# A new order of history copies, token sums, weight parts and snapshots around a blocked FFN-up product

## The chip, the cores and the metric

The kernel runs on one core of a Trainium2 chip. The metric is the device time of one execution in microseconds (us), given as the median of several runs. PE is the matmul engine (TensorE), DVE is VectorE, ACT is ScalarE, POOL is GpSimd, SP issues the weight DMAs.

## What is computed

Two layers of a streaming encoder over 512 prompt frames and 32 sample frames, handled together as 544 columns. Each layer has three gated branches (convolution, spatial gating, stick-breaking attention), an output projection with a layer norm, and then this channel mixer, in which the whole change lies:

```python
f_gate, f_val = jnp.split(x @ w_up, 2, axis=-1)          # 1024 -> 2 * 2816
ffn_ext = jnp.concatenate([ffn_hist, f_gate], axis=1)    # two frames of history
f = gelu(causal_dwconv(ffn_ext, ffn_conv_w, ffn_conv_b)) * f_val   # 3 taps
x = layer_norm(DN_ALPHA * x + f @ w_down, ln2_g, ln2_b)
```

## The kernel before

**Number format.** Every large product is made of three matmuls: an operand is split into a high part (ACT copies it to fp32r: `wh`, `xh`, `th`, `shi`, `fhh`) and a low part (DVE subtracts the high part from the raw value: `wl`, `xl`, `tl`, `slo`, `fll`). PE multiplies high by high, low by high and high by low. A weight chunk comes by DMA into one of three ring slots `raw`; `hi()` and `lo()` make its two parts (the low part takes the place of the raw values), and PE frees the slot when its last unit is read. The 544 columns are two halves of 272.

**The FFN-up product.** 22 gate tiles and 22 value tiles of 128 channels are made in pairs. The first two pairs of each are plain chunks: s0 (gate 0), s1 (value 0), s2 (gate 1), and one last plain chunk, value 1, which is the `chunk()` ahead of the blocked part. The other 18 weight chunks are 18 blocks q (`QUADS`), a gate chunk and a value chunk in turn, so that two blocks make one pair of tiles. A block is a 2 x 2 block product done with seven products (q,1) to (q,7) of 12 matmuls each instead of eight, in the Strassen-Winograd manner. Their order on PE is written out in `ORDER`: (q,3), (q,4), (q,5), (q+1,1), (q,6), (q+1,2), (q,7). For this

- POOL makes four sums of the activations once a layer (`traw` T1, T3, T2, T4N), and four sums of the weights for each block (`sums`, L558: s1, a21 in place, s2, s4);
- ACT makes their high parts (`turned_x_hi`, L979; `first_blocks`, `two_sums`, `last_sum`, L1007), and snapshots of PSUM banks between products (`snapshot`, L1012: m1, u1, u3), which PE must not overwrite before;
- DVE makes the low parts (`turned_x_lo`, L1791; `first_low`, L1798; `other_lows`, L1809: the second half of the weights, then `slo` in two pieces) and combines banks and snapshots (`bottom_right` c22, `left` c11 and c21, L1831). (q,7) waits for c22 of its block.

**Convolution of the gate.** `history` (DVE, L1764) puts two history columns into `gex`; `first_tap`, or `conv_open` (L967) for the plain pairs, applies the first tap on ACT; `conv_close` (DVE, L1746) the other two, with two small copies; ACT applies gelu; DVE multiplies with the values (`f_products`, `gated_values`). `gate_rows` (ACT, L962) copies plain gate rows from PSUM to `gex` and frees the bank.

**Down projection.** f is split by `f_his` (ACT, L1041) and `f_lows` (DVE, L1785) in six groups of tiles for each half of the columns. `down(h)` runs over six weight chunks, twice for each half; chunk j waits for its low part and for the f groups that it covers.

**What sets the order.** There is no planner: each engine has its own instruction list, written out in the code, and runs it strictly in that order; semaphores tie the lists together. An instruction that waits holds up all behind it on its engine.

## Time and profile before

| | us |
|---|---|
| median of three runs | 1814.01 (1813.14 to 1819.28) |
| the profiled execution, whole | 1812.31 |
| its span, first to last instruction | 1810.6 |
| PE busy | 1754.7 (97%) |
| DVE busy | 1348.9 (75%) |
| ACT busy | 850.5 (47%) |
| POOL busy | 345.0 (19%) |
| mean granted clock of PE | 0.991 |

The profile is of one execution. A row of the timeline gives start, length, engine, line, instruction, output and inputs, and in brackets how long the engine had been idle and what released it. The ends of matmuls are modelled and overlap, so the starts are the better guide: at full clock they are some 0.125 us apart. The granted clock is given as a share of 2.4 GHz; its other level is 1.2 GHz.

### The profile page before, as it was taken

To read this page: it belongs to the slowest core of one execution; us is meant where nothing else is said; L and a number is where in the kernel's file an instruction comes from. 1 tells how busy PE (TensorE), PEld (TensorE's weight loads), DVE (VectorE), ACT (ScalarE), POOL (GpSimd) and SP (SyncE) were. 2 spreads that over 40 slices of the span, in tenths; PEclk is the share of its full clock that TensorE was granted. 3 is DMA by queue.
4 is the path that set the end of the run, shared out by engine and by line. 5 is a ranking of instruction groups with operands and counts; after the bars stand their busy time and mean duration, and the time that the engine had idled before them with its cause. 6 is when DMAs were issued, how large, how long until landed. Compare 5 with 4: busy or idle time off the path is not lost.

```text
span 1810.6 us, 32645 instructions
## 1 busy us (share of the span) xinstructions
PE 1754.7 (97%) x13802; PEld 1709.7 (94%) x13802; DVE 1348.9 (75%) x1869; ACT 850.5 (47%) x1366; POOL 345.0 (19%) x311
## 2 busy tenths in 40 slices
PE   9999999999999999999999999999999999998997
PEld 9998999999999999999999989999999989998997
DVE  5798777755778888866668886786558778887665
ACT  4256523353455555544552564324535555555443
POOL 0034000000144455200000350000001545551000
PEclk9999999999999999999999999999999999999999
DMA  4522122223222222245525221222232222222544
GB/s 170 168 95 71 59 72 82 94 82 128 71 71 70 94 93 85 92 154 180 170 96 168 75 92 40 80 94 82 94 105 70 76 88 94 94 81 97 177 167 137
DMA packets 36514, 186.00 MB, mean 103 GB/s; under 512 B 7376, under 2 KB 11728, under 8 KB 18192
## 3 DMA queue, kind: packets, MB, share of 16 engines
q1 hardware_dynamic: 34672, 176.28, 29.0%
q10 hardware_dynamic: 1696, 7.64, 1.2%
q8 instruction: 109, 1.79, 0.4%
q14 instruction: 37, 0.30, 0.1%
HBM read 176.75 MB, written 7.15 MB: 102 GB/s over the span
## 4 chain that ended last, share of the span: by engine, by line
PE 74%; DVE 12%; issue 4%; DMA 4%; ACT 3%; POOL 3%; ACTq 0%; DVEq 0%; POOLq 0%
PE acc L1978 21%; PE acc L1984 20%; PE acc L1983 20%; DMA raw<-wup 3%; PE score L1978 2%; DVE slo L1818 2%; PE score L1984 2%; PE score L1983 2%; POOL sraw L569 1%; PE score L2054 1%; DVE wl L1199 1%; PE small L2105 1%; PE turned L2085 1%; DVE wl L1813 1%; DVE cbuf L1753 1%
## 5 line engine op out<-in xcount | busy, mean ns | idle before, releaser
L1978 PE MATMUL acc<-xh,wh 128*128 128x272 f32 x1936 | 570.6, 295 | 14.0 <-ACT gex L962 6.4
L1984 PE MATMUL acc<-xh,wl 128*128 128x272 f32 x1936 | 560.9, 290 | 0.0
L1983 PE MATMUL acc<-xl,wh 128*128 128x272 f32 x1936 | 559.9, 289 | 0.0
L1978 PEld LDWEIGHTS acc<-xh,wh 128*128 128x128 f32 x1936 | 367.5, 190 | 22.4 <-issue 18.3
L1199 DVE TENSOR_TENSOR wl<-raw,wh 128x2048 fp32r<-128x2048 f32 (+2 forms) x118 | 236.0, 2000 | 179.4 <-ACT wh L601 178.8
L1983 PEld LDWEIGHTS acc<-xl,wh 128*128 128x128 f32 x1936 | 367.7, 190 | 0.1
L1984 PEld LDWEIGHTS acc<-xh,wl 128*128 128x128 f32 x1936 | 366.7, 189 | 0.0
L601 ACT ACTIVATE wh<-raw 128x2048 fp32r<-128x2048 f32 (+2 forms) x138 | 236.4, 1713 | 169.1 <-DMA raw<-wdn 122.4
L1978 PE MATMUL acc<-fhh,wh 128*128 128x272 f32 x704 | 205.5, 292 | 6.2 <-DVE wl L1199 6.2
L1983 PE MATMUL acc<-fll,wh 128*128 128x272 f32 x704 | 203.5, 289 | 0.0
L1984 PE MATMUL acc<-fhh,wl 128*128 128x272 f32 x704 | 202.8, 288 | 0.0
L1403 DVE SCALAR_TENSOR_TENSOR acc<-glu,par,acc 128x574 f32<-128x574 f32 x240 | 181.0, 811 | 0.1
L1978 PEld LDWEIGHTS acc<-fhh,wh 128*128 128x128 f32 x704 | 133.2, 189 | 7.7 <-DVE wl L1199 7.3
L879 ACT ACTIVATE tmp<-acc,par 128x272 f32<-128x272 f32 x96 | 46.6, 488 | 195.5 <-PE acc L1984 195.2
L1984 PEld LDWEIGHTS acc<-fhh,wl 128*128 128x128 f32 x704 | 133.3, 189 | 0.0
L1983 PEld LDWEIGHTS acc<-fll,wh 128*128 128x128 f32 x704 | 133.0, 189 | 0.2
L546 POOL TENSOR_TENSOR wl<-raw,wh 128x512 fp32r<-128x512 f32 x8 | 11.3, 1440 | 593.2 <-ACT wh L601 593.2
L569 POOL TENSOR_TENSOR sraw<-raw 128x512 f32<-128x512 f32 x36 | 60.6, 1685 | 204.3 <-DMA raw<-wup 158.1
L1978 PE MATMUL score<-th,shi 128*128 128x272 f32 x288 | 85.4, 297 | 2.2 <-ACT u L1016 2.2
L1984 PE MATMUL score<-th,slo 128*128 128x272 f32 x288 | 83.5, 290 | 0.0
L1983 PE MATMUL score<-tl,shi 128*128 128x272 f32 x288 | 83.0, 288 | 0.0
L1818 DVE TENSOR_TENSOR slo<-sraw,shi 128x1024 fp32r<-128x1024 f32 x72 | 78.6, 1132 | 1.1 <-ACT shi L1005 1.1
(322 smaller groups left out, 4178.0 us busy)
## 6 DMA issues: line engine op xcount, KB each, us to landing
raw<-win SPq DMA_DIRECT2D x50, 1024.0 KB, 5.0
raw<-wup SPq DMA_DIRECT2D x44, 1024.0 KB, 4.9
raw<-wdn SPq DMA_DIRECT2D x32, 1024.0 KB, 4.9
raw<-wbr SPq DMA_DIRECT2D x24, 512.0 KB, 3.6
raw<-wdn SPq DMA_DIRECT2D x16, 768.0 KB, 4.2
raw<-wout SPq DMA_DIRECT2D x8, 1024.0 KB, 4.9
v_out<-vfm ACTq DMA_DIRECT2D x2, 1088.0 KB, 9.2
k_out<-k ACTq DMA_DIRECT2D x2, 1088.0 KB, 4.9
```

Source lines behind the costliest of these rows:

```text
L569: g.tensor_tensor(s1, a21, a22, ALU.add).then_inc(s_made, 1)
L601: A(wh[s][:, 0:n], raw[s][:, 0:n], ACT.Copy).then_inc(hi_full[s], c.up(hi_full[s]))
L879: A(tmp[:, b, :], ps[b][:, 0:HALF], ACT.Sigmoid, bias=col(par, PAR["b_gate"] + 8 * BRANCHES[n] + 2 * i + b % 2)).then_inc(acc_free[b], c.u ...
L1199: v.tensor_tensor(wl[s][:, 0:n], raw[s][:, 0:n], wh[s][:, 0:n].bitcast(F32), ALU.subtract).then_inc(lo_full[s], c.up(lo_full[s]))
L1403: v.scalar_tensor_tensor(out=acc[:, m, :], in0=glu_at(m, j), scalar=w, in1=acc[:, m, :], op0=ALU.mult, op1=ALU.add).then_inc(vec, c.up(vec))
L1753: v.scalar_tensor_tensor(out=cbuf[:, m, :], in0=gex[:, m, 1:GEX - 1], scalar=col(par, PAR["fw"] + FT + t), in1=cbuf[:, m, :], op0=ALU.mult ...
L1813: v.tensor_tensor(wl[s][:, n:], raw[s][:, n:], wh[s][:, n:].bitcast(F32), ALU.subtract).then_inc(lo_full[s], c.up(lo_full[s]))
L1818: v.tensor_tensor(slo[i][:, part, :], sraw[i][:, part, :], shi[i][:, part, :].bitcast(F32), ALU.subtract).then_inc(s_ready, 1)
L1978: first = mm(out, a, xs[0], start=start, stop=False, skip_group_check=onto)
L1983: mm(out, a, xs[1], start=False, stop=False, skip_group_check=onto)
L1984: return mm(out, b, xs[0], start=False, stop=stop, skip_group_check=onto)
L2054: last = mm(bs[b][:, 0:w], yc[x][rows, ht, i * P:w], ks[y][rows, ht, 0:w], start=x + y == 0, stop=y == 1)
```

## The change

It alters the written-out orders of ACT and DVE around the blocked part, one bank, and the waits of PE that go with it.

- Entry, ACT: the second pair's gate rows come ahead of the activation sums' high parts, which are made two (T2, T3) and later two (T1, T4N); the first taps of pair 1 (`conv_taps`) come ahead of block 0's weight parts, and the gelus of pair 1 behind block 0's sums.
- Entry, DVE: `history(1)` ahead of the last plain low part; two activation low parts; both tap groups of pair 1; then block 0's low parts, then the two other activation low parts. PE waits for each activation sum alone, where it is first used.
- Product (0,2) goes to the bank `bt` (`bank_of`), so it does not wait for the value products of pair 1; (1,2) and (2,2) do, and (1,4) waits for c11 of block 0.
- Loop, DVE: the history copy of the next pair comes right behind c11 of the even block instead of behind `other_lows` of the odd one; it also waits on `conv3_full`, which DVE's own taps raise.
- Loop, ACT: `last_sum(q + 1)` comes behind the snapshot u1 and, in odd q, behind the first taps.
- Exit: the first high and low parts of f move into the last turn of the loop, the down projection's second weight chunk is split ahead of the last gated values (DVE) and of f's third group; in the second half, each weight part comes ahead of the f part that it was behind.

```diff
--- before.py
+++ after.py
@@ -204,6 +204,7 @@
         TB = 4 * HALF * 4
         T2, T3, T1, T4N = range(4)
+        T_PLACE = {T2: 1, T3: 2, T1: 3, T4N: 4}
         th = [sb(f"th{j}", [P, 4, HALF], F32R, at=F + 2 * FB + 2 * j * TB) for j in range(4)]
         tl = [sb(f"tl{j}", [P, 4, HALF], F32R, at=F + 2 * FB + (2 * j + 1) * TB) for j in range(4)]
         traw = [sb(f"traw{j}", [P, 4, HALF], at=F + 2 * FB + (2 * j + 1) * TB) for j in range(4)]
@@ -371,6 +372,11 @@
         cbank = (bo, bt)
         PA, PB, PC = (ps[0], ps[1]), (bs[0], bs[1]), (bo, bt)
+        def bank_of(q, p):
+            if p == 2:
+                return PA[q % 2] if q else PC[1]
+            return (PC if p in (4, 7) else PB)[q % 2]
+
         def full_at(l, q, p):
             return l * len(ORDER) + PLACE[q, p]
@@ -964,21 +970,17 @@
                         A(gex[:, m, 2 + HALF:2 + SEQ], bank[:, 0:BP], ACT.Copy)
                         A(gex[:, m, 4 + SEQ:GEX], bank[:, BP:HALF], ACT.Copy).then_inc(acc_free[b], c.up(acc_free[b]))
-                def conv_open(i, later=0):
-
-                    act.wait_ge(acc_free[3], c.seen(acc_free[3], 1 if later else 0))
+                def conv_taps(i):
+                    act.wait_ge(acc_free[3], c.seen(acc_free[3]))
                     act.wait_ge(gex_full, c.take(gex_full, 2))
                     for m in range(2):
                         t = 2 * i + m
                         A(cbuf[:, m, :], gex[:, m, 0:GEX - 2], ACT.Identity, scale=col(par, PAR["fw"] + t),
                                    bias=col(par, PAR["fb"] + t)).then_inc(tap0_full, c.up(tap0_full))
-                    for m in range(2):
-                        act.wait_ge(conv3_full, c.take(conv3_full))
-                        A(cbuf[:, m, :], cbuf[:, m, :], ACT.Gelu).then_inc(fgelu_full, c.up(fgelu_full))
-
-                def turned_x_hi():
-                    for n, j in enumerate((T1, T3, T2, T4N)):
-                        act.wait_ge(t_made, 4 * l + n + 1)
+
+                def turned_x_hi(*js):
+                    for j in js:
+                        act.wait_ge(t_made, 4 * (l + 1))
                         A(th[j][:, :, :], traw[j][:, :, :], ACT.Copy).then_inc(t_hi, 1)
                 def chunk_of(q):
@@ -1053,22 +1055,29 @@
                 norm_out(1, "ln1_g", "ln1_b")
                 gate_rows(2, bs[0])
                 gate_rows(3, bs[1])
-                conv_open(0)
+                conv_taps(0)
+                conv_gelu(0)
+                conv_gelu(1)
                 hi()
                 for b in range(4):
                     c.skip(acc_full[b])
                     c.skip(acc_free[b])
-                turned_x_hi()
-                second_blocks(0)
-                for b in range(4):
+                for b in range(2):
                     gate_rows(b, SECOND_GATE[b])
+                turned_x_hi(T2, T3)
+                for b in range(2, 4):
+                    gate_rows(b, SECOND_GATE[b])
+                conv_taps(1)
                 for b in range(4):
                     c.skip(acc_full[b])
                     c.skip(acc_free[b])
+                second_blocks(0)
                 first_blocks(0)
-                conv_open(1, 1)
                 two_sums(0)
                 last_sum(0)
+                turned_x_hi(T1, T4N)
+                conv_gelu(0)
+                conv_gelu(1)
                 for q in range(QUADS + 1):
                     if q:
                         snapshot("u3", q - 1, 5, "c22")
@@ -1076,24 +1085,25 @@
                     if q < QUADS:
                         snapshot("m1", q, 1, "c11")
                     else:
-                        f_his(0, 1)
+                        f_his(0, 0)
                     if q and q % 2 == 0:
                         conv_gelu(0)
                     if q:
                         top_right(q - 1)
+                    if q == QUADS:
+                        f_his(0, 1)
                     first_blocks(q + 1)
                     if q and q % 2 == 0:
                         conv_gelu(1)
                     two_sums(q + 1)
-                    last_sum(q + 1)
                     if q == QUADS - 1:
                         hi()
                     if q < QUADS:
                         snapshot("u1", q, 3, "c21")
                     if q % 2:
                         first_tap(q - 1)
-                    if q == QUADS - 1:
-                        f_his(0, 0)
+                    last_sum(q + 1)
+                hi()
                 f_his(0, 2)
                 hi()
                 for g_ in range(3, 6):
@@ -1105,7 +1115,7 @@
                         hi()
                 final = l == DEPTH - 1
-                his(2)
+                his(1)
                 f_his(1, 0)
                 his(1)
                 f_his(1, 1)
@@ -1114,8 +1124,8 @@
                 his(1)
                 skip(range(4))
                 for g_ in range(3, 6):
+                    his(1)
                     f_his(1, g_)
-                    his(1)
                 his(1)
                 square_first(0)
                 his(2)
@@ -1763,6 +1773,8 @@
                 def history(i):
+                    if c.seen(conv3_full):
+                        dve.wait_ge(conv3_full, c.seen(conv3_full))
                     for m in range(2):
                         ins = v.tensor_copy(gex[:, m, 2 + SEQ:4 + SEQ], row(fhist, 2 * i + m, 0, 2))
                         ins.then_inc(gex_full, c.up(gex_full))
@@ -1788,10 +1800,10 @@
                     v.tensor_tensor(fll[h][:, a:b, :], f32[h][:, a:b, :], fhh[h][:, a:b, :].bitcast(F32),
                                     ALU.subtract).then_inc(f_ready, c.up(f_ready))
-                def turned_x_lo():
+                def turned_x_lo(*js):
                     dve.wait_ge(t_made, 4 * (l + 1))
-                    for n, j in enumerate((T1, T3, T2, T4N)):
-                        dve.wait_ge(t_hi, 4 * l + n + 1)
+                    for j in js:
+                        dve.wait_ge(t_hi, 4 * l + T_PLACE[j])
                         v.tensor_tensor(tl[j][:, :, :], traw[j][:, :, :], th[j][:, :, :].bitcast(F32),
                                         ALU.subtract).then_inc(t_ready, 1)
@@ -1830,7 +1842,7 @@
                 def left(q, m):
                     i = 2 + q // 2
-                    bank, add = (PA[q % 2], snap[q % 2]["m1"]) if m == 0 else (PC[q % 2], snap[q % 2]["u1"])
+                    bank, add = (bank_of(q, 2), snap[q % 2]["m1"]) if m == 0 else (PC[q % 2], snap[q % 2]["u1"])
                     dve.wait_ge(prod_full, full_at(l, q, 7 if m else 2))
                     dve.wait_ge(snapped, act_at(l, "u1" if m else "m1", q))
                     out = gex[:, m, 2:2 + HALF] if q % 2 == 0 else f32[0][:, 2 * i + m, :]
@@ -1850,36 +1862,41 @@
                 history(0)
                 conv_close(0)
                 f_products(0, FIRST_VALUE)
+                history(1)
                 lo()
-                turned_x_lo()
-                history(1)
-                first_low(0)
+                turned_x_lo(T2, T3)
                 skip(range(4))
                 conv_close(1, range(2), False)
+                first_low(0)
                 other_lows(0)
+                turned_x_lo(T1, T4N)
                 f_products(1)
+                history(2)
                 for q in range(QUADS + 1):
                     if q:
                         bottom_right(q - 1)
+                    if q == QUADS:
+                        f_lows(0, 0)
                     if q and q % 2 == 0:
                         conv_close(1 + q // 2, (1,), False)
                     if q < QUADS:
                         left(q, 0)
+                        if q and q % 2 == 0:
+                            history(2 + q // 2)
                     first_low(q + 1)
                     if q:
                         left(q - 1, 1)
+                    if q == QUADS:
+                        f_lows(0, 1)
+                        lo()
                     if q and q % 2 == 0:
                         gated_values(q - 1)
                     if q == QUADS - 1:
                         lo()
                     other_lows(q + 1)
                     if q % 2:
-                        history(2 + q // 2)
                         conv_close(2 + q // 2, (0,), False)
-                    if q == QUADS - 1:
-                        f_lows(0, 0)
-                for g_ in range(1, 3):
-                    f_lows(0, g_)
+                f_lows(0, 2)
                 lo()
                 for g_ in range(3, 6):
                     f_lows(0, g_)
@@ -1889,7 +1906,7 @@
                         lo()
                 final = l == DEPTH - 1
-                los(2)
+                los(1)
                 f_lows(1, 0)
                 los(1)
                 f_lows(1, 1)
@@ -1900,8 +1917,8 @@
                     residual(b, b, 0)
                 shift_sum(0)
                 for g_ in range(3, 6):
+                    los(1)
                     f_lows(1, g_)
-                    los(1)
                 centre(0)
                 lo()
                 squares_open()
@@ -2335,7 +2352,7 @@
                 def products(n):
                     q, p = ORDER[n]
-                    bank = {1: PB, 6: PB, 7: PC, 2: PA, 3: PB, 4: PC, 5: PB}[p][q % 2]
+                    bank = bank_of(q, p)
                     sums = 2 * (r * QUADS + q)
                     if p == 1:
                         blocks[q] = arrived()
@@ -2345,13 +2362,15 @@
                         pe.wait_ge(lo_full[blocks[q]], c.take(lo_full[blocks[q]]))
                         if q > 1:
                             pe.wait_ge(combined, dve_at(r, "c11", q - 2))
-                        else:
-                            pe.wait_ge(acc_free[q], c.seen(acc_free[q]))
+                        if q in (1, 2):
+                            pe.wait_ge(acc_free[q % 2], c.seen(acc_free[q % 2]))
                     if p == 3:
                         pe.wait_ge(snapped, act_at(r, "m1", q))
                         pe.wait_ge(s_ready, sums + 1)
-                        if q == 0:
-                            pe.wait_ge(t_ready, 4 * (r + 1))
+                    if p in (3, 4, 5, 7) and q == 0:
+                        pe.wait_ge(t_ready, 4 * r + T_PLACE[{3: T2, 4: T3, 5: T1, 7: T4N}[p]])
+                    if p == 4 and q == 1:
+                        pe.wait_ge(combined, dve_at(r, "c11", 0))
                     if p == 4 and q > 1:
                         pe.wait_ge(combined, dve_at(r, "c21", q - 2))
                     if p == 5:
```

## Rows read from the trace of the kernel before

**Rows 1.** The page: busy time, share of the span and instructions of each engine.

```profile
PE 1754.7 (97%) x13802; PEld 1709.7 (94%) x13802; DVE 1348.9 (75%) x1869; ACT 850.5 (47%) x1366; POOL 345.0 (19%) x311
```

**Rows 2.** The waits of PE: who for, us in total, times, longest.

```profile
PE score L1978 <- ACT u L1016: 21.4, 18, 2.5
PE acc L1978 <- ACT gex L962: 6.4, 2, 3.2
...
```

**Rows 3.** Timeline of PE: start, us, instruction, in brackets idle time before and releaser.

```profile
536.87 0.57 PE L1978 MATMUL acc<-xh,wh 128*128 128x272 f32 x1 [3.21 <-ACT gex L962]
...
555.82 0.36 PE L1978 MATMUL acc<-xh,wh 128*128 128x272 f32 x1 [2.51 <-DVE f L1777]
...
646.59 0.40 PE L1978 MATMUL score<-xh,shi 128*128 128x272 f32 x1 [1.14 <-ACT u L1016]
...
770.69 0.39 PE L1978 MATMUL acc<-fhh,wh 128*128 128x272 f32 x1 [2.12 <-DVE wl L1199]
...
806.28 0.39 PE L1978 MATMUL acc<-fhh,wh 128*128 128x272 f32 x1 [0.75 <-DVE wl L1199]
```

**Rows 4.** Stretches: length, PE, PEld, DVE, ACT, POOL busy (x), PEclk, DMA, GB/s.

```profile
521.47:533.49 12.02, 12.02 (x98) 11.96 (x96) 9.45 (x15) 8.45 (x11) 5.68 (x3) 1.00 0.51 174
536.87:551.64 14.77, 14.77 (x97) 14.77 (x97) 14.70 (x14) 4.02 (x9) 11.78 (x7) 0.80 0.21 72
646.59:669.79 23.20, 21.97 (x168) 21.31 (x168) 20.46 (x29) 12.86 (x22) 12.25 (x9) 1.00 0.26 93
770.69:780.00 9.31, 9.31 (x62) 9.31 (x63) 6.85 (x5) 3.42 (x3) 0.00 (x0) 0.82 0.39 124
```

**Rows 5.** Timeline of ACT at the entry.

```profile
531.40 4.09 ACT L982 ACTIVATE th<-traw 128x1088 fp32r<-128x1088 f32 x4
```

**Rows 6.** Timeline of DVE at the entry.

```profile
533.74 9.21 DVE L1795 TENSOR_TENSOR tl<-traw,th 128x1088 fp32r<-128x1088 f32 x4
...
544.11 1.21 DVE L1806 TENSOR_TENSOR wl<-raw,wh 128x1024 fp32r<-128x1024 f32 x1
```

**Rows 7.** Timeline of POOL at the entry.

```profile
542.48 1.62 POOL L569 TENSOR_TENSOR sraw<-raw 128x512 f32<-128x512 f32 x1 [0.68 <-DMA raw<-wup]
```

**Rows 8.** Timeline of ACT in a pair of blocks.

```profile
644.68 1.58 ACT L1034 ACTIVATE cbuf<-gex,par 128x546 f32<-128x546 f32 x2 [3.33 <-DVE gex L1767]
646.17 0.37 ACT L1016 ACTIVATE u<-score 128x272 f32<-128x272 f32 x1
```

**Rows 9.** Timeline of PE, first matmuls of (7,7) and (8,7).

```profile
649.98 0.39 PE L1978 MATMUL turned<-th,wh 128*128 128x272 f32 x1
...
660.93 0.29 PE L1978 MATMUL small<-th,wh 128*128 128x272 f32 x1
```

**Rows 10.** Timeline of DVE in the same pair.

```profile
644.34 0.23 DVE L1767 COPY gex<-fhist 128x2 f32<-128x2 f32 x2
...
647.87 1.71 DVE L1759 SCALAR_TENSOR_TENSOR cbuf<-gex,par,cbuf 128x546 f32<-128x546 f32 x1
...
649.50 0.43 DVE L1829 TENSOR_TENSOR f<-turned,u 128x272 f32<-128x272 f32 x1
...
651.49 0.79 DVE L1759 SCALAR_TENSOR_TENSOR cbuf<-gex,par,cbuf 128x546 f32<-128x546 f32 x1
...
656.63 2.92 DVE L1818 TENSOR_TENSOR slo<-sraw,shi 128x1024 fp32r<-128x1024 f32 x2
...
659.48 0.40 DVE L1826 TENSOR_TENSOR gex<-small,u 128x240 f32<-128x240 f32 x1
```

**Rows 11.** Timeline of POOL in the same pair.

```profile
644.72 1.28 POOL L569 TENSOR_TENSOR sraw<-raw 128x512 f32<-128x512 f32 x1 [4.62 <-DMA raw<-wup]
...
657.02 1.98 POOL L569 TENSOR_TENSOR sraw<-raw 128x512 f32<-128x512 f32 x1 [6.30 <-DMA raw<-wup]
```

**Rows 12.** Timeline of DVE at the end of the blocked part.

```profile
765.94 2.48 DVE L1788 TENSOR_TENSOR fll<-f,fhh 128x1088 fp32r<-128x1088 f32 x2
...
768.35 2.28 DVE L1199 TENSOR_TENSOR wl<-raw,wh 128x2048 fp32r<-128x2048 f32 x1
```

## The prediction

> **What bounds the kernel now.** I read the page's busy line first, then who PE waits for, then PE's instructions that follow an idle stretch, then the stretches around them. PE is busy for 1754.7 us, 97% of the span [rows 1], so an edit of order can only win idle PE time and the time in which PE runs below its full clock. The list of waits puts nearly all of the idle time in the blocked FFN-up part and its two ends [rows 2]: 21.4 us on ACT's snapshots in 18 waits and 6.4 us on ACT's gate rows in 2. In a layer these are: 3.21 us before the last plain value chunk, 2.51 us before product (0,2), 1.14 us before the sixth product of each odd block, 2.12 us and 0.75 us in the down projection [rows 3]. The stretches show the second loss: 96 products of matmuls take 12.02 us at granted clock 1.00, but 14.77 us behind the 3.21 us gap, where the clock is 0.80, that is partly at 1.2 instead of 2.4 GHz. Behind the 2.12 us gap 62 matmuls stand in 9.31 us at 0.82, where the full rate gives 74: 1.5 us lost. Behind the 1.14 us gaps the clock stays 1.00 [rows 4]. So a long gap costs about twice its length, a short one its length.
>
> **Entry, part by part.** PE's value chunk waits at 533.66 for ACT to empty two banks, and ACT first does four th copies (4.09 us from 531.40) and a weight half; the gate rows follow and end just before PE's start at 536.87 [rows 3, 5]. The change puts the gate rows ahead of the copies, at 531.4. Next in line is DVE's wl of that chunk, two instructions ahead of tl at 533.74 [rows 6], so PE starts at about 533.9, 2.9 us earlier, and loses no clock (14.77 - 12.02 = 2.7 us). The chunk ends at 546.0 instead of 551.6.
> What is late next is product (0,1). It wants the low half that DVE begins at 544.11 now, and the change puts that behind both tap groups. DVE and POOL are chained here: four tl take 9.21 us, and a conv tap needs 0.79 us alone and 1.71 us beside POOL [rows 6, 10]. I walk it with POOL at 1.25 us an operation: two tl end at 538.4, the first tap group's first instruction at 540.1, then block 0's last sum ends at 541.3, and block 1's four sums (now from 542.48, 5.6 us behind the chunk's first matmul, so then ready by 539.5) [rows 7] go in between the taps. The taps end at about 548.1, the low half at 549.3. PE waits from 546.0 to 549.4, 3.4 us, and I charge it the half clock behind it. (0,2) no longer waits for 2.51 us, because its bank is another one; the history copies and the two late tl lie where DVE has no one waiting. Of a 12-matmul product I take 1.5 us at full and 2.3 us at half clock: (0,1) and (0,2) end at 554.0, (0,3) at 555.5, and (0,4) starts there. It starts at 555.82 + 2.36 + 2.25 = 560.4 now. **Entry: 5.0 us a layer**; bounds 2 (a further POOL operation or two before the low half, one more clock loss) and 7 (no clock loss behind the new wait, and (2,5)'s wait for ACT, seen once a layer, gone).
>
> **The loop, 16 pairs of blocks in all.** The history copy moves ahead, so the first taps need not wait for it and ACT is free when (odd,5) ends; the last sum's high part moves behind the snapshot. Now ACT starts the taps at 644.68, 1.58 us long, and the snapshot that PE waits for comes behind it at 646.17 [rows 8]. In the new order the taps end about 1.3 us earlier, and the 1.14 us wait at (7,6) goes. But the wait behind it is already there: (7,7) starts at 649.98, and DVE's combination of the block before it ends at 649.50 + 0.43 = 649.93 [rows 9, 10]. That combination stands behind the conv taps of DVE, which alternate with POOL's four sums: 0.79 us alone, 1.71 us beside a sum. The sums start at 644.72, when the DMA lands [rows 11], and nothing in the change makes that earlier. So PE would do two products 1.1 us sooner and wait 1.1 us at (7,7). The union shows it from the other side: in a pair DVE is busy 20.46 us and POOL 12.25 us of 23.20 [rows 4]; DVE's idle pieces lie under POOL's operations, so together they leave some 0.2 us. PE's 168 matmuls need 21.0. Gain: the 0.15 us that the moved last sum holds back ACT's snapshot for (even,5). Cost: each history copy now stands between two instructions DVE is late with, 0.23 us, and the added wait on conv3_full is met in order on DVE, with the copy and the low half queued behind it. Bounds: 0.3 us a pair lost (DVE's slo at 656.63 starts only 0.39 us ahead of POOL's next sum at 657.02; 0.2 us later and a sum slips between) to 0.3 won. **Loop: 0, with +-5 us for both layers.**
> Here the Trainium skill bears (SBUF — State Buffer, "Who interferes with whom"): it states that VectorE and GpSimd share one port pair as an exclusive lock, taken for a whole instruction, and that a VectorE instruction with two SBUF inputs contends with a GpSimd one that reads SBUF. The stretched rows look like that. By it the loop gives nothing; were the engines independent, it would give all its waits back.
>
> **Exit.** ACT's first high part of f leaves the place ahead of the last snapshot, and DVE's moves behind its combination. (17,6) is then bound by (17,5) itself: 0.2 us. DVE's weight low part, which PE waits for, starts at 768.35 now, behind the three gated values and two f low parts (2.48 us from 765.94) [rows 12]. The change pulls it ahead of the gated values and of one of these low parts (half of 2.48 us), but puts another f low part and ACT's order in its way; walked through, ACT's high part ends at 767.1 and DVE's low part at 769.4 instead of 770.6. PE's gap shrinks from 2.12 us to about 1.1, and a 1.1 us gap shows no clock loss: 1.5 us more. **0.2 + 1.0 + 1.5 = 2.7 us a layer**, bounds 1 and 3.4.
> **Down projection.** One f low part (1.2 us) goes behind the weight low part that releases PE at 806.28 [rows 3], which then ends before PE wants it at 806.28 - 0.75 = 805.5: **0.8 us a layer**. What is queued behind, f's later parts, is wanted only in the next half.
>
> **Sum.** 5.0 + 2.7 + 0.8 = 8.5 us a layer, 17.0 for two. The profiled execution took 1812.3 us (1.7 us around its span); that less 17.0 is 1795.3. The median of the runs is 1.7 us above it, so I forecast 1814.0 - 17.0 = **1797 us**.
>
> **Rivals.**
> A, *the loop gives its waits back*: the chain at (odd,7) loosens because DVE, 1 us earlier at its taps, gets in ahead of POOL's first sum. For it: where the history copy starts now, at 644.34, DVE would be ready for its taps some 0.2 us later (the moved last sum), still ahead of POOL's 644.72 [rows 10, 11]. Against: DVE and POOL leave no room in the pair, and a PE that is early frees the weight slot early, so POOL's sums then fall into the low parts. 16 x 1.14 = 18.2 us more: 1779 us.
> B, *slower*: the history copy plus an early (odd,7) puts two of POOL's sums (1.25 us each) ahead of DVE's slo in every pair. (even,7) starts at 660.93 and its combination ends at 659.48 + 0.40 = 659.9 [rows 9, 10], 1.0 us of slack, so each pair costs 2.5 - 1.0 = 1.5 us, 16 pairs 24 us, against 17 won: 1821 us. It decides from 1.1 us a pair, that is pairs of 24.3 us. Against: one sum slips in easily, two would need POOL 1.6 us earlier than now.
> C, *the entry only moves its gap*: the low half behind the taps is later by two more POOL sums and f's products stand behind it, so PE starts earlier and waits longer. It does not do what its order says. Entry 5.0 falls to 1: 1797 + 8 = 1805 us. For it: DVE has no idle time from 533 to 552, and the change takes none of its work away.
>
> **How the numbers follow.** Forecast case 0.60 (1790 to 1804), A 0.20, C 0.14, B 0.06. The range leaves out B and half of A: 1779 to 1808. A measurement of this kernel can tell about 0.3%, 5.4 us, so faster means below 1808.6: forecast case and A nearly whole, and most of C, 0.87; same 0.09; slower 0.04.
>
> **What would show it.** Right: the gap before the value chunk under 0.5 us and clock 1.00 over it; a new wait of 3 to 4 us at (0,1) for DVE's low part, none at (0,2); no waits at (odd,6) but ones of about 1 us at (odd,7) or (even,5) for DVE or ACT, pairs still 23 us long; the gap in the down projection near 1.1 us at full clock. Wrong: pairs of 22 us (A) or 24.3 (B), or (0,4) later than 558 (C).

## The result, and the profile after

The changed kernel takes 1789.52 us, the median of 4 runs (1788.27 to 1793.3), against 1813.84 us for the kernel before in the same comparison: ratio 0.9863, 95% interval 0.9839 to 0.9887. That is 24.3 us less where 17.0 were forecast. The time lies inside the range of 1779 to 1808; the sign was right, and the saving was forecast 7 us too small. Between the two profiled executions it is 1812.3 - 1789.45 = 22.9 us, and the ledger below is made against that.

The profiled execution, busy time of each engine (the line that answers to [rows 1]):

```profile
span 1787.7 us, 32649 instructions
...
PE 1742.1 (97%) x13802; PEld 1700.6 (95%) x13802; DVE 1372.6 (77%) x1869; ACT 853.7 (48%) x1366; POOL 353.8 (20%) x311
```

PE has the same 13802 matmuls and is busy 12.6 us less. A matmul takes longer at the lower clock, so this is a sign of less time spent there, not of less work. DVE has the same 1869 instructions and is busy 23.7 us *more*. More of its instructions now run beside a POOL operation. That costs nothing as long as nobody waits for them.

Who PE waits for (total us, times, longest), against [rows 2]:

```profile
PE turned L1995 <- DVE f L1841: 9.5, 7, 1.5
PE score L1995 <- ACT u L1018: 7.6, 12, 1.4
PE score L1995 <- DVE wl L1818: 5.9, 2, 3.0
PE small L1995 <- DVE gex L1839: 5.6, 8, 0.7
```

The waits for ACT's snapshots fell from 21.4 to 7.6 us and those for the gate rows are gone from the head of the list. Three groups of waits for DVE stand in their place. Such a list alone would suggest that the blocked loop gained much. The lengths of the pairs say otherwise.

PE's instructions behind an idle stretch (start, us, instruction, in brackets the idle time and its releaser). The first, third and seventh are the value chunk, a `turned` product in the loop and the first weight chunk of the down projection. They answer to [rows 3]:

```profile
533.81 0.40 PE L1995 MATMUL acc<-xh,wh 128*128 128x272 f32 x1 [0.18 <-DVE wl L1209]
...
549.09 0.39 PE L1995 MATMUL score<-xh,wh 128*128 128x272 f32 x1 [2.95 <-DVE wl L1818]
...
574.92 0.39 PE L1995 MATMUL turned<-th,wh 128*128 128x272 f32 x1 [1.38 <-DVE f L1841]
...
648.38 0.39 PE L1995 MATMUL score<-th,shi 128*128 128x272 f32 x1 [0.56 <-ACT u L1018]
...
655.38 0.39 PE L1995 MATMUL small<-th,wh 128*128 128x272 f32 x1 [0.69 <-DVE gex L1839]
...
762.19 0.40 PE L1995 MATMUL acc<-fhh,wh 128*128 128x272 f32 x1 [1.00 <-DVE wl L1209]
...
1481.41 0.40 PE L1995 MATMUL turned<-th,wh 128*128 128x272 f32 x1 [1.55 <-DVE f L1841]
```

The wait for the gate rows shrank from 3.21 to 0.18 us, the one at (0,2) is gone, and a new one of 2.95 us stands at (0,1). In the loop, PE no longer waits at the sixth product of the odd block. In most pairs of layer 1 it waits at (even,5) and (even,7) (0.56 + 0.69 us a pair); in the first five pairs of layer 2 it waits once a pair, 1.4 to 1.55 us at (odd,7). The down projection's gap is 1.00 us where it was 2.12, and the 0.75 us gap in it is gone.

The stretches that answer to [rows 4], with the same columns (length; PE, PEld, DVE, ACT, POOL busy; granted clock; DMA; GB/s). They are the value chunk, the first products of block 0, one pair of blocks, and the start of the down projection:

```profile
533.81:545.97 12.16, 12.16 (x96) 12.11 (x96) 12.12 (x9) 8.72 (x14) 11.93 (x7) 1.00 0.26 88
549.09:562.00 12.91, 12.91 (x90) 12.91 (x91) 11.65 (x20) 5.86 (x11) 3.33 (x2) 0.87 0.25 83
632.35:655.38 23.03, 21.78 (x169) 21.30 (x169) 22.44 (x29) 12.84 (x22) 13.07 (x9) 1.00 0.27 92
762.19:772.00 9.81, 9.81 (x78) 9.81 (x79) 9.69 (x10) 5.84 (x6) 0.00 (x0) 1.00 0.56 188
```

The value chunk runs at the full clock (12.16 us instead of 14.77). The 2.95 us gap behind it has a price of its own: the granted clock is 0.87 over the next 12.9 us. A pair is 23.03 us long where it was 23.20, so the pair is unchanged. The down projection starts at full clock.

**The ledger**, from the starts of the same matmuls in both profiles:

| part | forecast, both layers | measured |
|---|---|---|
| entry, up to (0,4) | 10.0 | 5.2 + 4.9 = 10.1 |
| loop, (0,4) to (17,7) | 0 (bounds -5 to +5) | 201.9 - 199.7 and 203.3 - 199.3: 6.2 |
| exit and down projection | 7.0 | 4.5 + 2.0 = 6.5 |

The three together are 22.8 us, all that the profiles differ by. The wait at (17,6), which the forecast counted in the exit with 0.2 us a layer, lies in the measured loop. The loop is the term that was mis-sized.

### The profile page after: what moved, and what is told of

It is laid out like the page before. It is cut to its first block, busy times and chain, and to the rows that moved or that the text cites. A ratio compares the mean times of both kernels' runs of the same rounds, so it can differ in the third digit from the quotient of the medians.

```text
span 1787.7 us, 32649 instructions
## 1 busy us (share of the span) xinstructions
PE 1742.1 (97%) x13802; PEld 1700.6 (95%) x13802; DVE 1372.6 (77%) x1869; ACT 853.7 (48%) x1366; POOL 353.8 (20%) x311
## 4 chain that ended last, share of the span: by engine, by line
PE 76%; DVE 13%; issue 5%; POOL 2%; DMA 2%; ACT 1%; ACTq 0%; DVEq 0%; POOLq 0%
PE acc L1995 21%; PE acc L2001 21%; PE acc L2000 21%; DVE cbuf L1763 2%; DVE fst L1766 2%; DVE slo L1830 2%; PE score L1995 2%; DMA raw<-wup 2%; PE score L2001 2%; PE score L2000 2%; PE score L2071 1%; POOL sraw L575 1%; PE small L2122 1%; PE turned L2102 1%; POOL sraw L578 1%
## 5 line engine op out<-in xcount | busy, mean ns | idle before, releaser
L2001 PE MATMUL acc<-xh,wl 128*128 128x272 f32 x1928 | 555.5, 288 | 0.0
L1995 PEld LDWEIGHTS acc<-xh,wh 128*128 128x128 f32 x1928 | 363.1, 188 | 11.2 <-issue 5.0
L2000 PEld LDWEIGHTS acc<-xl,wh 128*128 128x128 f32 x1928 | 363.2, 188 | 0.1
L2001 PEld LDWEIGHTS acc<-xh,wl 128*128 128x128 f32 x1928 | 362.2, 188 | 0.0
L1830 DVE TENSOR_TENSOR slo<-sraw,shi 128x1024 fp32r<-128x1024 f32 x72 | 90.7, 1287 | 0.0
```

Source lines behind the costliest of these rows:

```text
L1830: v.tensor_tensor(slo[i][:, part, :], sraw[i][:, part, :], shi[i][:, part, :].bitcast(F32), ALU.subtract).then_inc(s_ready, 1)
L1995: first = mm(out, a, xs[0], start=start, stop=False, skip_group_check=onto)
L2000: mm(out, a, xs[1], start=False, stop=False, skip_group_check=onto)
L2001: return mm(out, b, xs[0], start=False, stop=stop, skip_group_check=onto)
```

## The experiments

**Theory**: DVE and POOL together fill the steady pair, so its length cannot change. The gain is in the entry and the exit. **Rival**: the loop's two moves (the history copy and the last sum's high part) give something back. Four kernels take the change apart, then four probe what sets the pair. Three more look for the source of the loop's gain, and a last one follows from what sets the pair.

### Each part alone, and all but the loop

`loop_only`: the kernel before with only the loop's edits, which are these.

```diff
                     two_sums(q + 1)
-                    last_sum(q + 1)
...
                         first_tap(q - 1)
+                    last_sum(q + 1)
...
                 def history(i):
...
+                    if c.seen(conv3_full):
+                        dve.wait_ge(conv3_full, c.seen(conv3_full))
...
                 f_products(1)
+                history(2)
...
                         left(q, 0)
+                        if q and q % 2 == 0:
+                            history(2 + q // 2)
...
                     if q % 2:
-                        history(2 + q // 2)
                         conv_close(2 + q // 2, (0,), False)
```

> The kernel before with the loop's edits alone: history copy behind c11 of the even block, the last sum's high part behind the snapshot and the first taps. My theory (VectorE and GpSimd fill each pair of blocks together, PE's wait only moves): pairs stay 23.0 us, the 1.14 us waits of (odd,6) go and waits of the same sum stand at (odd,7), or at (even,5) and (even,7). 1814 us, within 4, of which at most 3 less from the last pair of each layer, where GpSimd has no sums left. Rival (the waits were lost time of ACT's order): pairs of 21.9 us, 1796 us.

Measured: 1805.82 us (1803.93 to 1807.21), ratio 0.9955, 0.9938 to 0.9972. With the kernel before at 1813.56 that is 7.7 us, more than either the theory's 0 or its allowance of 3, and well short of the rival's 18. PE's waits moved as forecast:

```profile
PE small L1982 <- DVE gex L1829: 8.6, 11, 1.2
PE score L1982 <- ACT u L1016: 7.4, 14, 0.6
```

Most of its pairs are 22.6 to 23.0 us long, so the steady pair hardly changed. Its loops are 200.5 and 198.5 us long against 201.9 and 203.3, mainly by their last pair, 21.15 and 23.13 us against 23.59 and 25.36; one pair of 27.1 us took part of it back.

`entry_only` and `exit_only`: the kernel before with the edits of the entry, or of the exit and the down projection, alone. The core of each:

```diff
-                turned_x_hi()
-                second_blocks(0)
-                for b in range(4):
+                for b in range(2):
+                    gate_rows(b, SECOND_GATE[b])
+                turned_x_hi(T2, T3)
+                for b in range(2, 4):
...
+                conv_taps(1)
+                second_blocks(0)
...
-                    bank = {1: PB, 6: PB, 7: PC, 2: PA, 3: PB, 4: PC, 5: PB}[p][q % 2]
+                    bank = bank_of(q, p)
```

> The kernel before with the entry's edits alone (gate rows ahead of the sums' high parts, bank of (0,2), low parts two by two, taps ahead of block 0's low parts). My theory: 5.0 to 5.3 us a layer, as (0,4) shows in the changed kernel: 1814 - 10.5 = 1803.5 us. Rival (port-bound from 533 us on, so a gain at the entry is eaten in the loop): 1810 to 1814 us.

Measured: 1807.27 us (1805.88 to 1814.05), ratio 0.9971, 0.9951 to 0.9991: 6.3 us less, between the theory's 10.5 and the rival's 0 to 4. (0,4) comes 4.1 us earlier in layer 1 and another 4.9 in layer 2, against 5.0 to 5.3 expected in each. The loops behind are 202.1 and 205.7 us long (201.9 and 203.3 in the kernel before); in layer 2 two pairs of 25.5 and 25.4 us took part of the gain back, and 1.2 us were lost at the lower clock at 1103, outside the changed part. So the entry's gain is there, but the run does not bring it whole.

```diff
+                    if q == QUADS:
+                        f_lows(0, 0)
...
+                    if q == QUADS:
+                        f_lows(0, 1)
+                        lo()
...
-                los(2)
+                los(1)
```

> The kernel before with the edits behind the loop alone (first f parts into the last turn, second down chunk's low part ahead of the gated values, weight parts ahead of f parts). My theory: 0.3 + 1.1 + 1.6 us at the exit and 0.9 + 0.8 us in the two halves of the down projection, 4.7 us a layer: 1804.6 us. Rival (only the exit counts, the rest is hidden by PE's queue): 3 us a layer, 1808 us.

Measured: 1805.86 us (1803.79 to 1812.53), ratio 0.9959, 0.9944 to 0.9973: 7.7 us less, between the theory's 9 and the rival's 6.

`no_loop`: the changed kernel with the loop's edits taken back out. Only `history`'s wait on `conv3_full` stays, here and in `entry_only`; it waits for earlier taps of DVE itself.

```diff
                     two_sums(q + 1)
+                    last_sum(q + 1)
...
-                    last_sum(q + 1)
...
-                history(2)
...
-                        if q and q % 2 == 0:
-                            history(2 + q // 2)
...
+                        history(2 + q // 2)
```

> The changed kernel with the loop's edits undone. My theory: the steady pairs are 23.0 us either way, so at most the last pair's 1.4 to 1.7 us a layer is lost: 1789.5 + 3 = 1792.5 us, with the waits back at (odd,6). Rival (the loop's edits gave the 7 us that the forecast missed): 1796 us or more.

Measured: 1799.25 us (1794.84 to 1802.8), ratio 0.9918, 0.9894 to 0.9942. It is 9.7 us above the changed kernel; the rival's number came, not the theory's. It is also 14.3 us below the kernel before, and `entry_only` and `exit_only` together give 14.0, so the parts add up. The waits for the snapshots are back, and the longest of them is not a usual one. PE's list of waits, then PE, ACT, DVE and POOL around that wait:

```profile
PE score L1993 <- ACT u L1018: 23.9, 19, 4.3
```

```profile
714.06 0.40 PE L1993 MATMUL score<-xh,shi 128*128 128x272 f32 x1 [4.32 <-ACT u L1018]
...
712.15 1.58 ACT L1036 ACTIVATE cbuf<-gex,par 128x546 f32<-128x546 f32 x2 [5.76 <-DVE gex L1779]
...
710.74 1.29 DVE L1779 COPY gex<-fhist 128x2 f32<-128x2 f32 x2
...
700.13 1.30 POOL L575 TENSOR_TENSOR sraw<-raw 128x512 f32<-128x512 f32 x1 [8.35 <-DMA raw<-wup]
```

Read from the bottom: POOL's sums begin late, DVE's low parts that need them follow late, and the history copy stands behind them in DVE's order (and takes 1.29 us instead of 0.23, beside POOL). ACT's taps wait 5.76 us for it, PE's snapshot stands behind the taps, and the pair is 27.3 us long. In the new order the history copy stands ahead of those low parts, so the taps no longer wait for them.

### What sets a pair

Four edits of the changed kernel, each of one load on DVE or POOL. `s4_fill` writes a constant where POOL subtracts the fourth weight sum, so the products on that sum are not the reference's. `short_gate` gates 8 columns of each piece of f and leaves the rest ungated. `pool_more` adds one POOL subtraction a block into a spare tile. `copies_first` puts DVE's two small fst copies ahead of its first tap instead of between the taps.

```diff
-                    g.tensor_tensor(s4, a12, s2, ALU.subtract).then_inc(s_made, 1)
+                    g.memset(s4, 0.0).then_inc(s_made, 1)
```

> The changed kernel; GpSimd fills the fourth weight sum with zeros instead of subtracting, so the sixth products are left out in effect. The instruction stays, but reads no SBUF. Theory (VectorE and GpSimd share a port, and the pair of blocks is as long as both need it): each pair loses two of the port's holds of 1.25 us, limited by PE's 21.1 us: pairs of 21.2 to 21.8 us, 16 x 1.2 to 1.8 = 19 to 29 us less, 1760 to 1770 us. Rival (the ring of weight slots, its DMA and the first three sums set the pair; the fourth is not in that chain): pairs stay 23.0 us, 1789 us.

Measured: 1758.18 us (1757.12 to 1759.23), ratio 0.9702, 0.9682 to 0.9723. A pair, and the fill with DVE's instruction beside it:

```profile
645.20:666.40 21.20, 21.20 (x171) 21.20 (x170) 19.09 (x28) 12.87 (x21) 10.64 (x9) 1.00 0.30 100
```

```profile
646.67 0.53 POOL L582 MEMSET sraw<- 128x512 f32 x1
...
646.72 1.23 DVE L1818 TENSOR_TENSOR wl<-raw,wh 128x1024 fp32r<-128x1024 f32 x1 [0.86 <-POOL sraw L578]
```

With two POOL subtractions fewer, PE is busy 21.20 us of 21.20: the loop is at PE's own floor. The time is 2 us below the expected range: it is 31 us under the changed kernel, of which 25 lie in the two loops, the only place that the expectation counted. DVE's subtraction beside the fill takes 1.23 us, what it takes alone.

```diff
-                    v.tensor_tensor(f32[0][:, t, :], f32[0][:, t, :], cbuf[:, :, 0:HALF], ALU.mult)
+                    v.tensor_tensor(f32[0][:, t, 0:8], f32[0][:, t, 0:8], cbuf[:, :, 0:8], ALU.mult)
...
```

> The changed kernel; VectorE multiplies the gated values of the blocked pairs on 8 columns only (the rest of f stays ungated), some 1.1 us less of VectorE's time a pair, which is in no chain that leads to a weight slot. Theory (port and VectorE full): pairs of about 22.0 us, 16 us less, 1773 us. Rival (weight ring): 1789 us.

Measured: 1779.54 us (1777.91 to 1781.18), ratio 0.982, 0.9798 to 0.9842. Pairs of 22.1 us:

```profile
633.10:655.20 22.10, 21.54 (x170) 21.19 (x169) 20.39 (x28) 12.72 (x22) 11.98 (x9) 1.00 0.28 96
```

DVE's work shrank by about 1.1 us a pair and the pair by 0.93, as expected. The total fell by 10.0 us (7.8 by the ratios), not by the 15 that this makes in 16 pairs: the first pair of layer 1 is 27.1 us long, 4.4 us more than in the changed kernel.

```diff
+                    if q < QUADS - 1:
+                        pool.wait_ge(extra, c.seen(extra))
+                        g.tensor_tensor(spare[:, :].rearrange("p (t n) -> p t n", t=4), x_at[0][0][:, :, 0:P],
+                                        x_at[0][1][:, :, 0:P], ALU.subtract).then_inc(extra, c.up(extra))
```

> The changed kernel with one more GpSimd subtraction of 128x512 behind the fourth sum of each block, into a spare tile, on which nobody waits. GpSimd is busy 13.1 of 23.0 us, so it has room for two more. Theory (shared port full): pairs grow by up to 2 x 1.25 = 2.5 us, to 24.5 to 25.5 us, 24 to 40 us more, 1814 to 1830 us. Rival (weight ring or ACT's order sets the pair): 1789 us.

Measured: 1823.16 us (1821.72 to 1824.6), ratio 1.0061, 1.0039 to 1.0083. A pair:

```profile
641.40:666.00 24.60, 21.93 (x168) 21.26 (x168) 24.02 (x29) 12.72 (x22) 16.77 (x11) 1.00 0.26 87
```

The pair grew by 1.6 us, not by the 2.5 us that two operations of 1.25 us come to if each held DVE up in full. DVE did no more work, but is busy 24.02 us of 24.60 and POOL 16.77.

```diff
+                            copies(t, m)
...
-                        v.tensor_copy(row(fst, t, 0, 2), gex[:, m, SEQ:SEQ + 2]).then_inc(vec, c.up(vec))
-                        v.tensor_copy(row(fst, t, 2, 4), gex[:, m, GEX - 2:GEX]).then_inc(vec, c.up(vec))
```

> The changed kernel; VectorE's two small copies of the last gate columns go ahead of the first of its two taps in the blocked pairs, instead of between them. The port's load is the same, but one hand-over to GpSimd fewer lies between the taps, 1.1 us ahead of the combination that (odd,7) waits for. Theory (port full): nothing, 1789.5 within 3 us. Rival (what counts is how often the two take turns ahead of the combination): 1 us a pair, 1773 us.

Measured: 1787.66 us (1787.18 to 1792.61), ratio 0.9864, 0.9848 to 0.9881: no difference from the changed kernel that can be told. Its steady pairs are 22.7 us, 0.3 less, but it has three pairs of 25.9, 26.0 and 27.1 us, and the changed kernel has none.

These four bear out the theory on the steady pair from both sides. They also show, in `short_gate` and `copies_first`, that a shorter steady pair does not bring its whole gain, since some long pairs stay. The two long first pairs among them have a history. There PE kept its full clock at the entry and reached (0,4) 4.6 us behind (0,1) instead of 6.2. Then it waited 3.1 and 3.2 us at (1,7) for DVE, and ran at the lower clock behind that. What it had won at the entry was lost in the first pair.

### Where the loop's gain comes from

Loop lengths from (0,4) to (17,7) of the profiles, in us, layer 1 / layer 2:

```
history copy in its old place          history copy in its new place
before      201.9 / 203.3              after        199.7 / 199.3
entry_only  202.1 / 205.7              loop_only    200.5 / 198.5
exit_only   201.6 / 204.2              hist_only2   199.6 / 199.4
no_loop     205.3 / 203.7
```

Every loop of the left column is longer than every loop of the right: the means are 203.5 and 199.5. (`copies_first`, which also has the new place but moves two more copies, has 199.1 and 204.5, so the new place alone does not rule a long loop out.) The last pair, (14,7) to (16,7), is 24.2 us on the left and 22.4 on the right, and the seven ahead of it sum to 163.3 and 161.3. I suspected that the old order makes a late landing of a weight load dearer, as in `no_loop` at 700.13, and again in the last pair of layer 2 in the kernel before. There PE waits 2.54 us for the snapshot instead of 1.14, and then 1.4 us are lost at the lower clock:

```profile
1622.36 1.35 POOL L569 TENSOR_TENSOR sraw<-raw 128x512 f32<-128x512 f32 x1 [7.54 <-DMA raw<-wup]
...
1635.28 0.59 PE L1978 MATMUL score<-xh,shi 128*128 128x272 f32 x1 [2.54 <-ACT u L1016]
```

To test it, `late_before2` and `late_after2` put a 256 KB load ahead of the weight loads of blocks 7, 10, 13 and 16, in the kernel before and in the changed one.

```diff
+                if turn[0] % LAYER - 46 in (7, 10, 13, 16):
+                    if c.seen(held):
+                        sp.wait_ge(held, c.seen(held))
+                    sp.dma_start(spare[:, :], win[0, :, 0:512]).then_inc(held, c.up(held, 16))
```

> The kernel before; ahead of the weight chunks of blocks 7, 10, 13 and 16 of each layer SP issues one more load of 256 KB into a spare tile, so that 8 chunks land some 1 us or more later, by design and not by chance. Theory now (the loop's old order amplifies a late landing, because PE's snapshot on ScalarE stands behind the history copy and the low parts, and the gap then costs the clock too): 2 to 3 us an event, 16 to 24 us over the kernel before, 1830 to 1838 us. Rival (a late landing costs its own lateness, in either order): about 10 us, 1824 us.

Measured: 1821.09 us (1819.12 to 1823.57), ratio 1.005, 1.0033 to 1.0067: 7.5 us more, less than either the theory or its rival had. POOL's sums of those blocks start 6.3 to 7.8 us behind the last matmul that reads the slot, on average 1.5 us later than in the kernel before.

> The same eight late landings in the changed kernel. Theory now: its order takes them up, 0.5 to 1.5 us an event, 4 to 12 us over 1789.5, 1794 to 1801 us, so that the distance between the two kernels grows from 24 us to 30 us or more. Rival (the loop's edits gain by something else): the distance stays 24 us, 1800 us or what the kernel before with late landings gives, less 24.

Measured: 1805.75 us (1800.22 to 1807.85), ratio 0.9953, 0.9937 to 0.9969: 16.2 us more than the changed kernel, beyond the theory's 4 to 12. The sums start 6.3 to 8.0 us behind the free slot, on average 1.8 us later than in the changed kernel. Its PE waits on DVE in the loop:

```profile
PE turned L2001 <- DVE f L1847: 17.5, 7, 3.3
```

So the idea failed its test. The same late loads bring the two kernels nearer (24 us apart, then 15), not further apart; in sum the new order loses more by them.

The traces still leave a part of the idea open. In the profile of `late_after2`, 4 of the 14 us by which the loops are longer lie in the first pairs (24.6 and 25.0 us), ahead of the first late load; PE had kept its full clock at the entry there too. The last pair, with block 16 late, is 23.2 us in both layers there, but 23.8 and 25.7 in `late_before2`. And some blocks land late by themselves. Where the weights of an even block landed 6.1 to 6.6 us behind the free slot, its pair took 23.3, 24.0 and four times 25.4 to 25.5 us in the old order (`before`, `entry_only`, `exit_only`), and 23.0 to 23.4 us in four cases of the new one (`after`, `loop_only`, `hist_only2`). At 7.3 and 7.7 us both orders have a pair of 27: the one of `no_loop` above, and this one of `loop_only`, where PE waits at (odd,7), with a granted clock of 0.83 from 721.6 to 731.0:

```profile
719.04 0.59 PE L1982 MATMUL turned<-th,wh 128*128 128x272 f32 x1 [3.20 <-DVE f L1831]
```

This is read from seven traces, not tested: no run sets the lateness of one block alone.

`hist_only2` is the changed kernel with the last sum's high part back in its old place; of the loop's edits only the history copy's, with its wait, is left.

```diff
                     two_sums(q + 1)
+                    last_sum(q + 1)
...
-                    last_sum(q + 1)
```

> The changed kernel with the last sum's high part back ahead of the snapshot, so of the loop's edits only the moved history copy is left. Theory: the history copy is what held up the first taps and the snapshot behind them; the last sum cost 0.15 us a pair and hides elsewhere now: 1789.5 to 1792 us. Rival (both are needed, the last sum's wait for GpSimd holds up the snapshot): 1795 us or more.

Measured: 1789.12 us (1789.0 to 1789.41), ratio 0.987, 0.9855 to 0.9884. The loop's whole gain is the history copy's move. The move of the last sum's high part does nothing to the time that can be measured, though it changes whom PE waits for:

```profile
PE score L1995 <- ACT u L1018: 14.8, 15, 1.1
```

It is 7.6 us in 12 waits with that move, and the loops are 199.7 and 199.3 long instead of 199.6 and 199.4.

`act_copies2` follows from the pair's bound. In the pair of the changed kernel, a DVE copy of 2 columns stands between the taps and takes as long as a POOL operation:

```profile
642.87 1.46 DVE L1763 SCALAR_TENSOR_TENSOR cbuf<-gex,par,cbuf 128x546 f32<-128x546 f32 x1
644.26 1.25 DVE L1766 COPY fst<-gex 128x2 f32<-128x2 f32 x1
645.42 0.15 DVE L1767 COPY fst<-gex 128x2 f32<-128x2 f32 x1
```

The edit gives both copies of a tile to ACT, as one instruction ahead of ACT's tap.

```diff
+                        A(row(fst, t, 0, 4).rearrange("p (a b) -> p a b", a=2),
+                          gex[:, m, SEQ - 32:GEX].rearrange("p (a b) -> p a b", a=2)[:, :, 32:34], ACT.Copy)
...
-                        v.tensor_copy(row(fst, t, 0, 2), gex[:, m, SEQ:SEQ + 2]).then_inc(vec, c.up(vec))
-                        v.tensor_copy(row(fst, t, 2, 4), gex[:, m, GEX - 2:GEX]).then_inc(vec, c.up(vec))
```

> The changed kernel with the two small copies of the last gate columns made by one ScalarE copy a tile ahead of the first tap, instead of by VectorE between its taps. Theory (VectorE and GpSimd fill the pair): four VectorE copies of 0.16 us and their waits for GpSimd are gone, pairs of 22.4 to 22.7 us against 23.0, 16 x 0.3 to 0.6 = 5 to 10 us less, 1780 to 1785 us. Rival (ScalarE's first taps, now 0.4 us longer, hold up the snapshot at (odd,6)): 1789 us or more.

Measured: 1779.48 us (1778.17 to 1782.11), ratio 0.9818, 0.9803 to 0.9833. It is 34 us below the kernel before and 10 below the changed one. A pair, ACT's instructions, and PE's wait at (0,1):

```profile
652.00:674.30 22.30, 21.42 (x168) 21.20 (x168) 21.50 (x25) 13.14 (x24) 13.31 (x9) 1.00 0.28 96
```

```profile
546.95 0.39 PE L1997 MATMUL score<-xh,wh 128*128 128x272 f32 x1 [1.44 <-DVE wl L1820]
...
655.64 0.20 ACT L1038 ACTIVATE fst<-gex 128x4 f32<-128x4 f32 x1
655.74 0.84 ACT L1040 ACTIVATE cbuf<-gex,par 128x546 f32<-128x546 f32 x1
```

The steady pair is 22.3 us, 0.7 less. The entry gains too: the two 1.25 us copies are gone from ahead of the low half, PE waits 1.44 us at (0,1) instead of 2.95, and (0,4) starts at 552.31 instead of 555.25 (2.8 us more in layer 2). So of the 11 us between the two profiles some 5.7 are the entry's and 5.2 the loops'. The expectation had its 5 to 10 us from the pairs alone. The total came, to 0.5 us, but half of it from the entry, which the expectation did not have. Layer 2 still has three pairs of 23.1 to 23.2 us.

## Why the prediction was right, and where it was not

**The entry** went as it was walked. Forecast and measured: value chunk at 533.9, 533.81; its end at 546.0, 545.97; end of the low half at 549.3, 547.83 + 1.21 = 549.0; the wait at (0,1) 3.4, 2.95; (0,4) at 555.5, 555.25. The value chunk's clock loss (2.7 us) went and a new, smaller one came behind the new gap, as charged: 0.87 over 12.9 us. Rival C, that the gap only moves, needed (0,4) later than 558. This holds for layer 1, from whose rows it was worked out. In layer 2 the sum is right (4.9) but its pieces differ, which is luck: there the value chunk of the kernel before took 13.6 us, not 14.8, and the wait at (0,2) was 3.66 us, not 2.51. The low half in its new place:

```profile
546.11 1.79 DVE L1769 SCALAR_TENSOR_TENSOR cbuf<-gex,par,cbuf 128x546 f32<-128x546 f32 x1
547.83 1.21 DVE L1818 TENSOR_TENSOR wl<-raw,wh 128x1024 fp32r<-128x1024 f32 x1
```

**The steady pair** was rightly put at no gain, by the argument of the union. Taken from both engines' timelines, DVE or POOL is busy in 22.73 of 23.02, 23.05 of 23.20 and 22.83 of 22.98 us of three pairs of the kernel before. The 1.14 us waits at (odd,6) went and others of about that size or somewhat more came: 0.56 us at (even,5) and 0.69 at (even,7), or 1.55 us at (odd,7). The forecast named (even,5) and (odd,7), not (even,7); its own walk, a wait of 1.1 us at (odd,7) in every pair, fits layer 2 better than layer 1. Rival A would need pairs of 22 us and B of 24.3; `short_gate` and `pool_more` reach about those lengths, by taking load away or adding it, and the change does neither.

**The loop as a whole** is the term that was mis-sized: 0, with +-5 us for both layers, against 6.2 us in the profile. That is why the total, 1789.5 us, lies just below the 1790 to 1804 us of the forecast case, though it is inside the range. The two pairs of runs that differ in the loop's edits alone give 7.7 (`loop_only`) and 9.7 us (`no_loop`). The step that failed is "16 pairs in all": it took one steady pair of [rows 4] for all. The last pair is another case, here in layer 1 of the kernel before and of the changed one (columns as above):

```profile
730.20:753.80 23.60, 21.95 (x171) 21.29 (x170) 19.75 (x28) 12.46 (x21) 8.10 (x6) 1.00 0.24 79
```

```profile
724.50:746.70 22.20, 21.64 (x169) 21.38 (x170) 20.18 (x28) 11.72 (x21) 7.96 (x6) 1.00 0.26 84
```

POOL has 6 operations in it instead of 9, 8.1 us instead of 12.25. DVE or POOL is busy in 20.80 of 23.59 us there, so the union no longer fills the pair, and an order that lets the taps start sooner can pay: 23.59 and 25.36 us became 22.16 and 22.17, 4.6 of the 6.2 us. Some 1.8 of these 4.6 us are chance as much as order. Layer 2's 25.36 us hold the 2.54 us wait and the clock loss shown above, behind weights that landed 6.5 us after their slot was free; in the changed kernel those of this block took 5.5. Block 17's end behind it is 0.3 us shorter a layer; that is the (17,6) wait (0.78 us, then 0.49), which the forecast had as 0.2 in the exit. The last 1.0 us is spread over the seven pairs ahead in each layer. The long pairs (24 to 27 us) add to it in some kernels of the old order and in fewer of the new. What decides how often they come is not settled: late landings, injected, hurt the new order more in sum, while the ones that came by themselves were mostly dearer in the old. Two such pairs are shown, at 714.06 and 719.04; most others have a shorter wait, of 2.5 us. A faster landing could not be tried apart from other changes.

**Exit and down projection**: 7.0 forecast, 6.5 measured, with two errors that cancel. The low part that PE waits for ends 7.1 us behind (17,7) where 7.0 was worked out, and the gap is 1.00 us where 1.1 was said:

```profile
757.58 1.28 DVE L1800 TENSOR_TENSOR fll<-f,fhh 128x1088 fp32r<-128x1088 f32 x1
759.84 2.29 DVE L1209 TENSOR_TENSOR wl<-raw,wh 128x2048 fp32r<-128x2048 f32 x1 [0.98 <-ACT wh L607]
762.05 0.72 DVE L1857 TENSOR_TENSOR f<-f,cbuf 128x544 f32<-128x544 f32 x1
```

But the 1.5 us for the clock were charged to both layers from a row of layer 1. In layer 2 of the kernel before, the stretch behind the same gap (2.13 us, at 1667.31) had its full rate:

```profile
1667.31:1676.70 9.39, 9.39 (x75) 9.39 (x76) 6.83 (x5) 3.43 (x3) 0.00 (x0) 1.00 0.55 177
```

So 1.5 us of the forecast were not there to win: layer 2 gained 2.0 us, layer 1 4.5. In layer 1 a 0.46 us wait in the second half of the projection (at 874.63) went as well. That was worth some 0.85 us, which the sum did not have, and makes up for part of the error.

## What to carry to other kernels

Where two engines share a resource, sum their busy time as a union over one period before judging an order: 88% and 53% alone hid some 99% together. A new order did not shorten the steady period; moving four copies of 0.15 us each to a third engine did. Read every period of a loop, the last one and the longest ones too, before multiplying a steady one by their count. And where a price comes from a stretch of one layer, look at the same stretch in the other.

## What the runs showed of the hardware

- **A tiny DVE copy can cost a whole POOL operation.** The copy of 128x2 takes 0.15 us alone and 1.25 us where POOL subtracts beside it; a conv tap 0.79 and 1.5 to 1.8 us; a weight low half of 128x1024 1.21 to 1.23 and 2.35 us. DVE's combinations out of the accumulators stay at 0.43 us. A POOL fill (0.53 us) held nobody up. This is the exclusive lock of the Trainium skill (SBUF — State Buffer, "Who interferes with whom"), and the trace agrees; that even the smallest instruction pays the rest of the POOL operation is what I had not expected.
- **What load on either engine is worth in a pair**: about 1.1 us of DVE work less, 0.93 us less; two POOL subtractions less, 1.8 us less, and then PE's own 21.2 us are the bound; two more, 1.6 us more.
- **The clock after a gap is not one function of the gap.** 3.21 us of idle: 0.80 over 14.8 us. 2.95 us: 0.87 over 12.9 us. 2.12 us: 0.82 over 9.3 us in one layer, 1.00 in the other. 2.30 us (`exit_only`, at 1516.32): 1.00. The gaps of 1.55 us and less that are shown here had 1.00 behind them.
- **A landing varies**: POOL's first sum of a block starts mostly 5.0 to 6.0 us behind the last matmul that reads the slot, at times 6.1 to 7.7 us with no load added. It is often the same block: block 14 of layer 1 took 6.4 us in `before`, 6.6 in `entry_only`, 7.3 in `no_loop` and 7.7 in `loop_only`. Pairs of 24 to 27 us stand on the late ones in some cases.
